# Differential attention: mixing the two softmax maps before the first one is normalized

## The chip, the cores and the metric

The kernel runs on one core of a Trainium2 chip. The core has a matmul engine (PE, with its weight loads shown apart as PEld), a vector engine (DVE), an activation engine (ACT), a general engine (POOL) and an engine that issues transfers (SP). Each works through its own queue of instructions in order, and they meet at semaphores. The metric is the device time of one execution, in microseconds.

## The reference, cut to what matters

The whole program is a chain of four layers. The change touches the attention of the first layer: 512 tokens (256 of the context, 256 of the image), 4 heads, and in each head two pairs of queries and keys, 64 wide, that give two maps over the same values.

```
def _diff_softmax_mix(q, k, v, lam):
    s = jnp.einsum('bhmqd,bhmkd->bhmqk', q.astype(F32), k.astype(F32)) * (A_QK_DIM ** -0.5)
    p = jax.nn.softmax(s, axis=-1)
    w = p[:, :, 0] - lam * p[:, :, 1]
    return jnp.einsum('bhqk,bhkd->bhqd', w, v.astype(F32))
...
    k_all = jnp.concatenate([k_c.astype(F32), k_l], axis=3)
```

`lam` is one number, computed from four small inputs. Written with unnormalized exponentials e0, e1 and their sums s0, s1 over the keys, the mixture is w = e0 / s0 - lam * e1 / s1.

## The kernel before

The program is a row of stages; between two stages all engines meet. The stage in question is `diff_attention_stage` (from L2593). It walks through 16 units (h, q): head h of 4, block q of 4 with 128 queries each. Blocks 0 and 1 see all 512 keys, blocks 2 and 3 only the last 256 (`first_key`). All data is float32.

For each unit, and each on its engine:
- `score` (PE, L2642): two products, one for each map, queries of the block against the keys, into banks 2 * (u % 2) + m.
- `maxima` (DVE, L2722, L2723): the row maxima of both maps, times the negative scale.
- `exps` (ACT, L2686): the exponentials of both maps into `prob`, with their row sums in columns 2 and 3 of `stat`.
- L2736 to L2738 (DVE): inverses of the two sums into columns 4 and 5; the second times `net.LAM` (which holds minus lam); the second map times this column, in place. `link` makes DVE wait for its own last instruction.
- L2742 (DVE): first map times column 4, plus the second map: `mixed`.
- L2668 (PE): `mixed` is transposed in tiles of 128x128 into bank 4 + u % 2, by `nc.tensor.transpose` with the identity matrix of the constants.
- L2702 (ACT): the bank is copied to `mixed_t`.
- `weigh` (PE, L2652): values times `mixed_t`, summed over key tiles into bank 6; once a head DVE copies the bank to `OT` (L2751, the last one L2754).

The order is written out by hand in each engine's loop. PE runs scores two units ahead and weighs one unit behind:

```
            for u, (h, q) in enumerate(units):
                if u + 2 < len(units):
                    score(u + 2)
                pe.wait_ge(mixed_ready, u + 1)
...
                if u:
                    weigh(u - 1)
                for n in hosted[u]:
                    mod.add(pe, n, first_slot)
```

The stage hosts other work in its gaps. `Modulation` streams the matrices of the layers' modulation, 1 MB at a time, through a ring of four places: SP fetches (L432) when PE has used a place; `mod.add` on PE first folds the sums before (`fold`, L456) and then takes one block (L443, 16 small products); `mod.copy` on ACT (L451) brings the sums out of the bank. Three blocks come before unit 0 and then one for each of the units 1 to 15. ACT copies the block of unit u - 1 at the start of its loop for unit u. Besides, POOL sums neighbouring tokens for the next stages (L2628 to L2631) in the first part of the stage, ACT damps a tile (L2710) and DVE adds them (`shift`, L2729), from unit 2 and 3 on. In the loop of unit u ACT's order is: modulation copy, copy of the turned mixture of u, exponentials of u + 2, damping. DVE's order is: inverses and mixture of u, maxima of u + 2, shift, and the copy of the output where a head ends.

Of the kernel before, what the change touches and what calls it, by code (L numbers as in the profile page):

```python
# [29 lines left out]
ALU = mybir.AluOpType  # L30
ACT = mybir.ActivationFunctionType
# [3 lines left out]
P = 128  # L35
# [3 lines left out]
TOK = 512  # L39
# [14 lines left out]
C_IDENT, C_ONES, C_BLK, C_LE, C_GE = (P * n for n in range(5))  # L54
# [2538 lines left out]
def diff_attention_stage(net, mod, first_slot, last_slot):  # L2593
# [4 lines left out]
    nc = net.nc  # L2598
    near = [net.HT[:, t, :] for t in range(KT)] + [net.PT[:, t, :] for t in range(26, 32)]
    values = net.SC[:, 0:2048].rearrange("p (t m) -> p t m", m=512)  # L2600
    prob = net.SC[:, 2048:4096].rearrange("p (b m k) -> p b m k", b=2, m=2)
    mixed = net.SC[:, 4096:5120].rearrange("p (b k) -> p b k", b=2)
    mixed_t = net.SC[:, 5120:6144].rearrange("p (b k) -> p b k", b=2)
    stat = net.SC[:, 6144:6144 + 8 * 16].rearrange("p (u n) -> p u n", n=8)
    units = [(h, q) for h in range(4) for q in range(NCH)]
    first_key = lambda q: 0 if q < 2 else 2
    scale = 64 ** -0.5
    with Stage(net, "diff_attention") as st:
        scored, max_ready, exp_ready = st.sem("scored"), st.sem("max_ready"), st.sem("exp_ready")
        mixed_ready, turned, turned_copied = st.sem("mixed_ready"), st.sem("turned"), st.sem("turned_copied")  # L2610
        out_ready, out_taken, own = st.sem("out_ready"), st.sem("out_taken"), st.sem("dve_own")
        near_ready, damped = st.sem("near_ready"), st.sem("damped")
        ahead = range(first_slot, first_slot + 3)
        upto = [first_slot + 3 + (last_slot - first_slot - 2) * u // 16 for u in range(len(units) + 1)]
        hosted = [range(upto[u], upto[u + 1]) for u in range(len(units))]

        @st.sync
        def _(sp):
            for n in range(first_slot + SLOTS, last_slot + SLOTS + 1):
                sp.wait_ge(mod.summed, n - SLOTS + 1)  # L2620
                mod.fetch(sp, n)
# [11 lines left out]
        @st.tensor  # L2633
        def _(pe):
            def score(u):
                h, q = units[u]
                if u >= 2:
                    pe.wait_ge(exp_ready, 2 * (u - 1))
                k0 = first_key(q) * P
                for m in range(2):  # L2640
                    rows = slice(64 * m, 64 * m + 64)
                    last = nc.tensor.matmul(net.ps[2 * (u % 2) + m][:, k0:TOK], net.PT[rows, h, P * q:P * q + P],  # L2642
                                            net.PT[rows, 4 + h, k0:TOK], start=True, stop=True)
                last.then_inc(scored, 1)

            def weigh(u):
                h, q = units[u]
                pe.wait_ge(turned_copied, u + 1)
                if q == 0 and h:
                    pe.wait_ge(out_taken, h)  # L2650
                for t in range(first_key(q), NCH):
                    last = nc.tensor.matmul(net.ps[6][:, P * q:P * q + P], values[:, t, P * h:P * h + P],  # L2652
                                            mixed_t[:, u % 2, P * t:P * t + P],
                                            start=(t == first_key(q)), stop=(t == NCH - 1))
                last.then_inc(out_ready, 1)

            score(0)
            score(1)
            for n in ahead:
                mod.add(pe, n, first_slot)  # L2660
            for u, (h, q) in enumerate(units):
                if u + 2 < len(units):
                    score(u + 2)
                pe.wait_ge(mixed_ready, u + 1)
                if u >= 2:
                    pe.wait_ge(turned_copied, u - 1)
                for t in range(first_key(q), NCH):
                    last = nc.tensor.transpose(net.ps[4 + u % 2][:, P * t:P * t + P],  # L2668
                                               mixed[:, u % 2, P * t:P * t + P], net.const(C_IDENT))
                last.then_inc(turned, 1)  # L2670
                if u:
                    weigh(u - 1)
                for n in hosted[u]:
                    mod.add(pe, n, first_slot)
            weigh(len(units) - 1)
            mod.fold(pe, last_slot, first_slot)

        @st.scalar
        def _(act):
            def exps(u):  # L2680
                k0 = first_key(units[u][1]) * P
                act.wait_ge(max_ready, u + 1)
                if u >= 2:
                    act.wait_ge(mixed_ready, u - 1)
                for m in range(2):
                    act.activation(prob[:, u % 2, m, k0:TOK], net.ps[2 * (u % 2) + m][:, k0:TOK], ACT.Exp,  # L2686
                                   bias=stat[:, u, m:m + 1], scale=scale,
                                   accum_out=stat[:, u, 2 + m:3 + m]).then_inc(exp_ready, 1)

            mod.copy(act, ahead[0])  # L2690
            exps(0)
            mod.copy(act, ahead[1])
            exps(1)
            mod.copy(act, ahead[2])
            for u, (h, q) in enumerate(units):
                k0 = first_key(q) * P
                for n in hosted[u - 1] if u else ():
                    mod.copy(act, n)
                act.wait_ge(turned, u + 1)
                if u >= 2:  # L2700
                    act.wait_ge(out_ready, u - 1)
                act.activation(mixed_t[:, u % 2, k0:TOK], net.ps[4 + u % 2][:, k0:TOK],  # L2702
                               ACT.Copy).then_inc(turned_copied, 1)
                if u + 2 < len(units):
                    exps(u + 2)
                t = u - 2
                if t >= 0:
                    f = net.PT[:, 12 + t, :]
                    act.wait_ge(near_ready, 3 * (t + 1))
                    act.activation(f, f, ACT.Copy, scale=net.DER[:, 14 + t:15 + t]).then_inc(damped, 1)  # L2710
            for n in hosted[-1]:
                mod.copy(act, n)

        @st.vector
        def _(dve):
            link = Chain(dve, own)

            def maxima(u):
                k0 = first_key(units[u][1]) * P
                dve.wait_ge(scored, u + 1)  # L2720
                for m in range(2):
                    link(nc.vector.reduce_max(stat[:, u, m:m + 1], net.ps[2 * (u % 2) + m][:, k0:TOK], AX_X))  # L2722
                nc.vector.tensor_scalar(stat[:, u, 0:2], stat[:, u, 0:2], -scale, None,  # L2723
                                        ALU.mult).then_inc(max_ready, 1)

            def shift(t):
                f = net.PT[:, 12 + t, :]
                dve.wait_ge(damped, t + 1)
                nc.vector.scalar_tensor_tensor(f, near[t], net.DER[:, t:t + 1], f, ALU.mult, ALU.add)  # L2729

            maxima(0)
            maxima(1)
            for u, (h, q) in enumerate(units):
                k0 = first_key(q) * P
                dve.wait_ge(exp_ready, 2 * (u + 1))
                link(nc.vector.reciprocal(stat[:, u, 4:6], stat[:, u, 2:4]))  # L2736
                link(nc.vector.tensor_tensor(stat[:, u, 5:6], stat[:, u, 5:6], net.LAM[:, 0:1], ALU.mult))
                link(nc.vector.tensor_scalar(prob[:, u % 2, 1, k0:TOK], prob[:, u % 2, 1, k0:TOK],  # L2738
                                             stat[:, u, 5:6], None, ALU.mult))
                if u >= 2:  # L2740
                    dve.wait_ge(turned, u - 1)
                nc.vector.scalar_tensor_tensor(mixed[:, u % 2, k0:TOK], prob[:, u % 2, 0, k0:TOK], stat[:, u, 4:5],  # L2742
                                               prob[:, u % 2, 1, k0:TOK], ALU.mult, ALU.add).then_inc(mixed_ready, 1)
                if u + 2 < len(units):
                    maxima(u + 2)
                t = u - 3
                if t >= 0:
                    shift(t)
                if q == 0 and h >= 1:
                    dve.wait_ge(out_ready, 4 * h)  # L2750
                    nc.vector.tensor_copy(net.OT[:, h - 1, :], net.ps[6][:, :]).then_inc(out_taken, 1)  # L2751
            shift(len(near) - 1)
            dve.wait_ge(out_ready, len(units))
            nc.vector.tensor_copy(net.OT[:, 3, :], net.ps[6][:, :])  # L2754
            for some in ((first_slot, 23), (24, last_slot)):
                mod.bias(dve, (first_slot, last_slot), *some)
# [1433 lines left out]
```

## Time and profile before

| What | Value |
|---|---|
| median of 3 runs | 2049.76 us (2048.55 to 2051.72) |
| profiled execution | 2046.13 us |
| its span in the profile | 2044.3 us |
| PE busy in the span | 1846.4 us (90%) |
| DVE busy | 1245.1 us (61%) |
| ACT busy | 860.7 us (42%) |
| POOL busy | 285.4 us (14%) |
| mean granted clock of PE | 0.968 |
| the stage `diff_attention` | from 201.0 to 275.4 us |

Busy time is that of instructions in flight; matmuls overlap, so a busy PE is not PE at its peak. Most of the program is large matmuls in other stages; the stage of the change is 3.6% of the span. Times in the rows are counted from the span's start.

### The profile page before, as it was taken

What the parts mean: (1) busy time and instruction counts of PE and PEld (TensorE: products, weight loads), DVE (VectorE), ACT (ScalarE), POOL (GpSimd) and SP (SyncE); (2) the same over time, 40 slices, a digit from 0 to 9 for tenths busy, and PEclk for the clock granted to TensorE, in tenths of its full rate; (3) what the DMA queues carried; (4) which work ended last, traced back from release to release, by engine and by line L of the source; (5) the groups of instructions that cost most, each with busy time, mean ns of one, the idle gap of its engine ahead of it and who ended that gap; (6) DMA issues with size and microseconds to landing.
All of it is one profiled execution on the core that took longest, in us unless ns stands there. A gap on an engine that the chain in (4) does not pass through costs nothing. (4 is left out here: it accounts for less than half of the span.)

```text
span 2044.3 us, 42257 instructions
## 1 busy us (share of the span) xinstructions
PE 1846.4 (90%) x18096; PEld 1613.2 (79%) x18096; DVE 1245.1 (61%) x2155; ACT 860.7 (42%) x1592; POOL 285.4 (14%) x341
## 2 busy tenths in 40 slices
PE   7998787667789999999999779999889999979997
PEld 5786545556659888888978679999679999769997
DVE  4565857465565642453565868855667756667743
ACT  4321567335243321221334555534554445464432
POOL 0200303305113000002200420012021012021001
PEclk8999987989989999999999999999999999999998
DMA  9752751020052323232331055555225556225543
GB/s 319 207 165 83 229 171 36 4 64 4 4 176 72 108 98 97 89 103 83 108 100 41 22 187 182 189 187 165 83 83 191 181 167 205 83 83 180 190 149 101
DMA packets 249004, 255.04 MB, mean 125 GB/s; under 512 B 6914, under 2 KB 247186, under 8 KB 248690
## 3 DMA queue, kind: packets, MB, share of 16 engines
q1 hardware_dynamic: 239214, 242.85, 36.9%
q10 hardware_dynamic: 8740, 8.51, 1.3%
q8 instruction: 143, 2.34, 0.5%
q0 software_dynamic: 864, 0.98, 0.4%
q14 instruction: 43, 0.35, 0.1%
HBM read 251.28 MB, written 1.05 MB: 123 GB/s over the span
## 5 line engine op out<-in xcount | busy, mean ns | idle before, releaser
L529 DVE TENSOR_TENSOR RING_rounded<-RING,SC_rounded 128x1024 fp32r<-128x1024 f32 (+2 forms) x390 | 461.3, 1225 | 217.6 <-ACT SC_rounded L522 217.3
L549 PE MATMUL bank<-OT_rounded,SC_rounded 128*128 128x256 f32 (+1 forms) x1808 | 574.6, 318 | 15.1 <-DVE HT_rounded L1113 6.8
L550 PE MATMUL bank<-HT_rounded,SC_rounded 128*128 128x256 f32 (+1 forms) x1808 | 569.7, 315 | 0.0
L551 PE MATMUL bank<-OT_rounded,RING_rounded 128*128 128x256 f32 (+1 forms) x1808 | 568.0, 314 | 0.0
L522 ACT ACTIVATE SC_rounded<-RING 128x1024 fp32r<-128x1024 f32 (+2 forms) x390 | 372.5, 1006 | 329.9 <-DMA RING<-in_l_mlp_w 185.0
L549 PEld LDWEIGHTS bank<-OT_rounded,SC_rounded 128*128 128x128 f32 x1808 | 342.4, 189 | 45.0 <-DVE HT_rounded L1113 7.6
L551 PEld LDWEIGHTS bank<-OT_rounded,RING_rounded 128*128 128x128 f32 x1808 | 341.6, 189 | 25.4
L550 PEld LDWEIGHTS bank<-HT_rounded,SC_rounded 128*128 128x128 f32 x1808 | 342.1, 189 | 21.7
L549 PE MATMUL bank<-PT_rounded,SC_rounded 128*128 128x256 f32 (+1 forms) x896 | 277.6, 310 | 4.8 <-DVE RING_rounded L529 4.8
L550 PE MATMUL bank<-PT_rounded,SC_rounded 128*128 128x256 f32 (+1 forms) x896 | 277.2, 309 | 0.0
L551 PE MATMUL bank<-PT_rounded,RING_rounded 128*128 128x256 f32 (+1 forms) x896 | 275.9, 308 | 0.0
L549 PEld LDWEIGHTS bank<-PT_rounded,SC_rounded 128*128 128x128 f32 x896 | 168.5, 188 | 16.7 <-DVE RING_rounded L529 6.0
L551 PEld LDWEIGHTS bank<-PT_rounded,RING_rounded 128*128 128x128 f32 x896 | 168.2, 188 | 10.6
L550 PEld LDWEIGHTS bank<-PT_rounded,SC_rounded 128*128 128x128 f32 x896 | 168.4, 188 | 9.5
L550 PE MATMUL bank<-OT_rounded,SC_rounded 128*128 128x256 f32 (+1 forms) x336 | 101.4, 302 | 0.0
L549 PE MATMUL bank<-HT_rounded,SC_rounded 128*128 128x256 f32 (+1 forms) x272 | 84.4, 310 | 15.3 <-DVE OT_rounded L1464 6.6
L3349 DVE TENSOR_TENSOR SC<-SC,bank 128x512 f32<-128x512 f32 (+1 forms) x80 | 51.3, 683 | 68.0 <-PE bank L3230 67.5
L795 DVE SCALAR_TENSOR_TENSOR XT<-bank,MOD,XT 128x256 f32<-128x256 f32 x48 | 21.3, 479 | 115.3 <-PE bank L551 115.3
L551 PE MATMUL bank<-HT_rounded,RING_rounded 128*128 128x256 f32 (+1 forms) x272 | 83.2, 306 | 0.0
L775 ACT ACTIVATE PT<-bank 128x512 f32<-128x512 f32 x32 | 18.9, 598 | 123.7 <-PE bank L551 123.7
L549 PEld LDWEIGHTS bank<-HT_rounded,SC_rounded 128*128 128x128 f32 x272 | 52.6, 193 | 19.1 <-DVE RING_rounded L529 12.2
L836 DVE TENSOR_TENSOR PT<-PT 128x512 f32<-128x512 f32 x32 | 22.1, 690 | 74.7 <-ACT PT L775 74.7
(561 smaller groups left out, 2787.8 us busy)
## 6 DMA issues: line engine op xcount, KB each, us to landing
RING<-in_l_mlp_w SPq DMA_DIRECT2D x64, 1024.0 KB, 5.3
RING<-in_w_ffn_in SPq DMA_DIRECT2D x44, 1024.0 KB, 5.1
RING<-in_l_mod_w SPq DMA_DIRECT2D x32, 1024.0 KB, 6.1
RING<-in_l_w_in SPq DMA_DIRECT2D x25, 1024.0 KB, 5.4
RING<-in_w_ffn_out SPq DMA_DIRECT2D x16, 768.0 KB, 4.3
RING<-in_w_in SPq DMA_DIRECT2D x10, 1024.0 KB, 5.4
RING<-in_w_ffn_out SPq DMA_DIRECT2D x16, 640.0 KB, 3.9
PT<-in_l_mod_w SPq DMA_DIRECT2D x8, 1024.0 KB, 10.1
```

What stands on the lines that cost most here:

```text
L522: act.activation(net.high4(s, m)[:, 0:self.w.kts[s], :], net.ring_half(net.RING, s, m, self.w.kts[s]), ACT.Copy).then_inc(self.high_ready, 1)
L529: net.nc.vector.tensor_tensor(low, whole, net.high4(s, m)[:, 0:self.w.kts[s], :].bitcast(F32), ALU.subtract).then_inc(self.split_ready, 1)
L549: net.nc.tensor.matmul(bank[:, tokens], high, x_high, start=start, stop=False)
L550: net.nc.tensor.matmul(bank[:, tokens], high, x_low, start=False, stop=False)
L551: return net.nc.tensor.matmul(bank[:, tokens], low, x_high, start=False, stop=stop)
L775: act.activation(hidden.whole[:, 2 * q + m, :], part.bank(q, m)[:, :], ACT.Relu).then_inc(part.taken, 1)
L795: return nc.vector.scalar_tensor_tensor(into, bank[:, tokens], net.MOD[:, gate + tile, j:j + 1], into, ALU.mult, ALU.add)
L836: link(nc.vector.tensor_tensor(whole, whole, whole, ALU.mult))
L3349: nc.vector.tensor_tensor(inv, inv, bank, ALU.subtract).then_inc(doubled, 1)
```

## The change

The mixture is taken as s0 * w instead of w: with r = -lam * s0 / s1 it is e0 + r * e1, so the second map no longer needs a pass of its own, and both maps stay unnormalized. The factor 1 / s0 belongs to a row of the mixture, that is to a column of the turned one. It is applied while the mixture is turned: instead of a transpose with the identity, PE multiplies `mixed` with a diagonal matrix that holds 1 / s0. ACT makes this matrix for each unit (identity times column 4 of `stat`) in one of two new buffers, `scaling`, when DVE has signalled the inverses (`inverted`); PE waits for it (`scaling_ready`) in front of the turning. On DVE, the product of the second inverse and lam takes the first sum as a further factor.

```
+    scaling = net.SC[:, 6272:6528].rearrange("p (b m) -> p b m", b=2)
...
+        inverted, scaling_ready = st.sem("inverted"), st.sem("scaling_ready")
...
+                pe.wait_ge(scaling_ready, u + 1)
                 pe.wait_ge(mixed_ready, u + 1)
                 if u >= 2:
                     pe.wait_ge(turned_copied, u - 1)
                 for t in range(first_key(q), NCH):
-                    last = nc.tensor.transpose(net.ps[4 + u % 2][:, P * t:P * t + P],
-                                               mixed[:, u % 2, P * t:P * t + P], net.const(C_IDENT))
+                    last = nc.tensor.matmul(net.ps[4 + u % 2][:, P * t:P * t + P], mixed[:, u % 2, P * t:P * t + P],
+                                            scaling[:, u % 2, :], start=True, stop=True)
...
                 for n in hosted[u - 1] if u else ():
                     mod.copy(act, n)
+                act.wait_ge(inverted, u + 1)
+                act.activation(scaling[:, u % 2, :], net.const(C_IDENT), ACT.Copy,
+                               scale=stat[:, u, 4:5]).then_inc(scaling_ready, 1)
                 act.wait_ge(turned, u + 1)
...
                 dve.wait_ge(exp_ready, 2 * (u + 1))
-                link(nc.vector.reciprocal(stat[:, u, 4:6], stat[:, u, 2:4]))
-                link(nc.vector.tensor_tensor(stat[:, u, 5:6], stat[:, u, 5:6], net.LAM[:, 0:1], ALU.mult))
-                link(nc.vector.tensor_scalar(prob[:, u % 2, 1, k0:TOK], prob[:, u % 2, 1, k0:TOK],
-                                             stat[:, u, 5:6], None, ALU.mult))
+                nc.vector.reciprocal(stat[:, u, 4:6], stat[:, u, 2:4]).then_inc(inverted, 1)
+                dve.wait_ge(inverted, u + 1)
+                link(nc.vector.scalar_tensor_tensor(stat[:, u, 6:7], stat[:, u, 5:6], net.LAM[:, 0:1], stat[:, u, 2:3],
+                                                    ALU.mult, ALU.mult))
                 if u >= 2:
                     dve.wait_ge(turned, u - 1)
-                nc.vector.scalar_tensor_tensor(mixed[:, u % 2, k0:TOK], prob[:, u % 2, 0, k0:TOK], stat[:, u, 4:5],
-                                               prob[:, u % 2, 1, k0:TOK], ALU.mult, ALU.add).then_inc(mixed_ready, 1)
+                nc.vector.scalar_tensor_tensor(mixed[:, u % 2, k0:TOK], prob[:, u % 2, 1, k0:TOK], stat[:, u, 6:7],
+                                               prob[:, u % 2, 0, k0:TOK], ALU.mult, ALU.add).then_inc(mixed_ready, 1)
```

## Rows read from the trace of the kernel before

**Rows 1.** Stretches (us): busy us of each engine (records), granted clock, DMA share, GB/s.

```profile
215.00:220.00 5.00, 2.50 (x12) 2.50 (x13) 4.83 (x8) 1.35 (x5) 5.00 (x12) 0.60 0.26 90
...
250.00:275.00 25.00, 22.25 (x228) 15.60 (x228) 20.35 (x50) 15.50 (x41) 0.00 (x0) 1.00 0.85 275
```

**Rows 2.** Waits, 195 to 285 us: who, for whom, total us, times, longest.

```profile
PEld bank L2668 <- DVE SC L2742: 17.5, 12, 4.7
```

**Rows 3.** Waits of SP's queue, 195 to 290 us.

```profile
SPq L432 <- PE bank L443: 73.5, 19, 12.7
```

**Rows 4.** Groups of instructions, 200 to 277 us: busy us, mean ns, idle before.

```profile
L2652 PE MATMUL bank<-SC 128*128 128x128 f32 x96 | 14.3, 288 | 0.0
...
L2668 PE MATMUL bank<-CONST,SC 128*128 128x128 f32 x48 | 9.2, 304 | 11.6 <-DVE SC L2742 11.6
L2738 DVE TENSOR_SCALAR SC<-SC 128x512 f32<-128x512 f32 (+1 forms) x16 | 8.7, 541 | 0.6
```

**Rows 5.** Timeline of PE, steady part: start us, us, engine, line, records [idle before].

```profile
250.73 0.66 PE L2668 MATMUL bank<-CONST,SC 128*128 128x128 f32 x4 [0.74 <-DVE SC L2742]
...
251.22 1.06 PE L2652 MATMUL bank<-SC 128*128 128x128 f32 x8
...
254.61 0.44 PE L2668 MATMUL bank<-CONST,SC 128*128 128x128 f32 x2
...
254.88 1.06 PE L2652 MATMUL bank<-SC 128*128 128x128 f32 x8
...
256.21 1.07 PE L443 MATMUL bank<-RING,SC 128*32 128x256 f32 x16
...
257.21 1.13 PE L2642 MATMUL bank<-PT 64*128 64x512 f32 x4
...
258.27 0.44 PE L2668 MATMUL bank<-CONST,SC 128*128 128x128 f32 x2
...
266.12 0.66 PE L2668 MATMUL bank<-CONST,SC 128*128 128x128 f32 x4 [0.74 <-DVE SC L2742]
...
271.55 0.44 PE L2668 MATMUL bank<-CONST,SC 128*128 128x128 f32 x2
```

**Rows 6.** Timeline of ACT and DVE, the same part.

```profile
251.42 0.60 ACT L2702 ACTIVATE SC<-bank 128x512 f32<-128x512 f32 x1 [1.43 <-PE bank L2668]
...
252.81 0.73 ACT L2710 ACTIVATE PT<-PT,DER 128x512 f32<-128x512 f32 x1
...
254.73 1.42 DVE L2722 TENSOR_REDUCE SC<-bank 128x1 f32<-128x512 f32 x2 [1.23 <-PE bank L2642]
...
256.38 0.69 ACT L2686 ACTIVATE SC<-bank,SC 128x512 f32<-128x512 f32 x1 [0.91 <-DVE SC L2723]
...
257.72 0.71 ACT L2710 ACTIVATE PT<-PT,DER 128x512 f32<-128x512 f32 x1
...
258.33 0.38 ACT L451 ACTIVATE SC<-bank 128x256 f32<-128x256 f32 x1
```

**Rows 7.** Groups of ACT by shape, whole execution.

```profile
L3714 ACT ACTIVATE PT<-bank,LORA 128x128 f32<-128x128 f32 x16 | 4.8, 445 | 0.0
...
L3743 ACT ACTIVATE RING<-RING 128x128 f32<-128x128 f32 x4 | 1.6, 394 | 0.0
...
L1769 ACT ACTIVATE PT<-bank 128x128 f32<-128x128 f32 x4 | 1.1, 280 | 30.1 <-PE bank L1704 30.1
```

**Rows 8.** Timeline of DVE and PE, first units.

```profile
208.69 1.45 DVE L2738 TENSOR_SCALAR SC<-SC 128x512 f32<-128x512 f32 x1
...
211.89 0.66 PE L2668 MATMUL bank<-CONST,SC 128*128 128x128 f32 x4 [1.55 <-DVE SC L2742]
...
217.50 1.12 PE L2668 MATMUL bank<-CONST,SC 128*128 128x128 f32 x4 [4.32 <-DVE SC L2742]
...
223.83 0.44 PE L2668 MATMUL bank<-CONST,SC 128*128 128x128 f32 x2
...
227.49 0.44 PE L2668 MATMUL bank<-CONST,SC 128*128 128x128 f32 x2
```

## The prediction, made before the changed kernel ran

> **What bounds the kernel now.** The change sits in one stage, so I read that stage alone. First the busy time of each engine in it: between 250 and 275 us PE is busy 22.25 of 25 us and DVE 20.35, ACT only 15.50 [rows 1]. Two engines are nearly full and the third has room on average; averages don't say which one a step waits for, so next come the waits: PE's weight loads stood 17.5 us before the turning (L2668), always for the mixture of DVE (L2742) [rows 2]. Weights from memory are no limit: SP waits 73.5 us for PE to free a place of the ring, and the DMA engines are at 0.85 [rows 1, 3].
>
> Then the timeline, for the order of work. One unit (a head, a block of queries) takes on PE: score two units ahead, turn, weigh the unit before, fold, add. A head has two units with 512 keys ("wide") and two with 256 ("narrow"). From the turn of 250.73 (unit 9) to that of 266.12 (unit 13), one head, it is 15.39 us [rows 5]: 3.88 to the turn at 254.61, 3.66 to the one at 258.27, and 7.85 for the last two steps. PE's own work fills the first two. In the turn at 266.12 the row itself names DVE's mixture as what was waited for. ACT never sets the pace.
>
> **The change, part by part.**
>
> *Removed: a pass of DVE over the second map.* L2738, 16 times, 8.7 us busy together [rows 4]. Two of them are drawn out at the start (1.45 us, [rows 8]); the others have 0.41 on average, 1.7 us in a head. PE would get its mixture that much earlier. That is a gain only where nothing else is late next.
>
> *Exchanged on DVE: a product on one column for another with a second factor.* Same engine, same tiny shape; I take no difference, and a few hundredths of a microsecond at 16 units either way stay below 1 us.
>
> *PE: matmuls in place of transposes.* A transpose leaves one record (48 in L2668), a product of the same shape two (96 in L2652 for 48 products) [rows 4]. Four transposes move the following work on by 0.49 us (250.73 to 251.22); eight records of L2652 and the four of the fold take 1.33 (254.88 to 256.21); then add takes 1.00 and a wide score 1.06 [rows 5]. Of the 1.33 I count 0.44 for the fold's four, so 0.89 for eight product records, 0.11 each. With 0.06 for the first pair, a wide turn becomes 0.95 instead of 0.49, a narrow one 0.50 instead of 0.28 (254.61 to 254.88): plus 0.46 and 0.22, or 1.4 us a head. Bounds: nothing, if this operand streams as in a transpose; and the whole of it, since shape and type are those of L2652, which is why I take it.
>
> The Trainium skill (TensorE: Matmul & The Clock Gate, Terms) calls transpose mode four times faster for FP32. The rows make it twice: 0.11 us for a transposed tile, 0.22 for a multiplied one. By the rule the change would cost 0.33 us for each of 48 tiles, by the rows 0.11.
>
> *ACT: a diagonal for each unit*, a 128x128 activation. The row nearest in form (SBUF to SBUF) is 0.394 us, one from a bank is 0.280, one with a column for its bias 0.445 [rows 7]. I take 0.39 to its end and 0.30 to the next start, as activations overlap by a tenth (the damping of 257.72 lasts 0.71 and the next starts 0.61 later [rows 6]). In ACT's queue it stands behind the copy of the modulation rows (L451), which waits for PE's add, and behind the exponentials and the damping (L2710). The turn now waits for this chain. That is what is late next.
>
> I lay one head out. ACT's chain after a wide turn: turn 0.95, end of the last product and hand-over 0.20 (the same as 251.42 less 251.22), copy and two narrow exponentials 1.39 (251.42 to 252.81), damping 0.61, rows copied 0.29, diagonal 0.39, hand-over 0.06: 3.89 us [rows 5, 6]. After a wide score DVE is slower: its maxima start 1.18 us after the score does (the score starts 1.06 before the turn of 254.61, the maxima at 254.73), the exponentials at 256.38, the damping at 257.72; with 0.61, 0.29, 0.39 and 0.06 this is 5.52 us from the score's start, 4.46 from turn to turn [rows 5, 6]. Each step takes the longer of this and of PE's own chain:
> - step 1, wide to narrow: PE 0.95 + 0.89 + 0.44 + 1.00 + 1.06 = 4.34, ACT 3.89. It was 3.88.
> - step 2, narrow to narrow: PE 0.50 + 0.89 + 0.44 + 1.00 + 1.06 = 3.89, ACT 4.46. It was 3.66.
> - step 3, narrow to wide: PE under 3.5; the score went out 4.46 - 2.83 = 1.63 us before the turn, so ACT 5.52 - 1.63 = 3.89.
> - step 4, wide to wide: PE 3.9 at most, ACT 3.89. Steps 3 and 4 were 7.85 together.
>
> Together 16.6 instead of 15.39: plus 1.2 us a head. From the turn of unit 3 on: two heads 2.4; steps 3 and 4 once more, -0.1. The last two units have no score to hide the diagonal, for the rows can be copied only when add has ended: 0.95 + 0.89 + 0.44 + 1.12 + 0.29 + 0.45 = 4.14 and 0.50 + 0.89 + 0.44 + 1.12 + 0.29 + 0.45 = 3.69, against 5.43 for both (266.12 to 271.55): 2.4. The last turn: 0.2. **The later part loses 4.9 us.** With the diagonal at 0.28 it is 4.1, at 0.445 it is 5.2.
>
> *The start gains.* While POOL is busy (5.00 of 5 us in [rows 1]), DVE's passes are drawn out: L2738 took 1.45 us at 208.69 [rows 8]. Units 0 and 1 each drop one. The first turn moves from 211.89 to about 210.5, the second from 217.50 to 214.6. The turn of unit 2 came 6.33 us after it, at 223.83, where the laid-out step is 4.34: the granted clock was 0.60 between 215 and 220 us, that is 4 of 5 us at the 1.2 GHz level, from about 216.0; PE had stood idle 4.32 us before the turn of 217.50 [rows 1, 8]. After the change this idle time is about 2.3 us (210.5, 0.95 for the turn, some 0.8 for a narrow score). Bounds:
> - the slow stretch stays where it was: from 214.6 to 216.0 at full clock, the other 2.94 at half, so turn 2 at 221.9 and turn 3 4.4 later, at 226.3 instead of 227.49: gain 1.2;
> - it goes: turn 2 at 214.6 + 4.34 = 219.0, turn 3 at 223.4: gain 4.0.
>
> An idle time of 1.55 us before the turn of 211.89 was followed by work at full clock, the one of 4.32 by the fall; 2.3 is nearer to the first, but not by so much that I leave the second out. I take 3.1.
>
> *Small things.* Two more semaphores to clear on POOL when the stage ends, one more wait in PE's queue a unit, mostly passed while PE works: 0 to 0.8 us, taken as 0. The stages behind only start later.
>
> **The sum.** 4.9 - 3.1 = +1.8 us, between +0.9 and +3.7. The profiled execution took 2046.13 us (span 2044.3), so 2047.9; the median of the runs, 2049.76, lies 3.6 above it, so in its terms 2051.6. A measurement of this kernel can tell about 0.2%, 4.1 us, from nothing.
>
> **Rivals.**
> - *DVE was the bound and its relief counts (faster).* The waits for the mixture [rows 2] speak for it. It needs both new costs gone: products at the pace of transposes, the diagonal ready before the score ends. Then steps 3 and 4 fall by about 0.7 us a head to ACT's old chain, 1.7 in the later part, and with 4.0 at the start this is -5.7: 2044. It decides from the point where ACT's chain is 0.6 us shorter than laid out. Against it: the two records of L2652. 12 in 100.
> - *ACT's chain longer, slow stretch unchanged (slower).* A diagonal of 0.5 us and 0.1 us more of waits a unit on PE and ACT give 6.5 in the later part, less 1.2: +5.3, 2055. For it: every link of the chain is a hand-over between engines. 22 in 100, with all else beyond +4.1 but the next.
> - *A product four times a transpose.* As a mechanism: 0.44 us a tile for 0.11, a wide turn 1.8, a narrow one 0.93. PE's chain then sets every step but one, a head takes 18.7 us and the later part loses 11.5, the start gains 2.5: +9, 2059. The records of L2652 [rows 4] deny it; the rule quoted above would have it so. 4 in 100.
> - *The forecast*, all between -1.9 and +4.1: 62 in 100. Its lower end has the diagonal hidden and the products paid (later part +2.1, start -4.0).
>
> So faster by over 0.2%: 0.12; within it: 0.62; slower: 0.26. The range for 8 in 10 runs from 2046 to 2056, from inside the faster rival to just above the slower one; the forecast's own is 2048 to 2054.
>
> **What would show it.** Right: 96 PE records of the turning, a wide turn as x8 of about 1.06 us; in the waits PE stands before the turning for ACT, no more for DVE; a head takes 16.6 us; the turn of unit 1 is at 214.6. Wrong: PE still waits for L2742, or the diagonal is ready before the score ends (then faster), or it lasts 0.5 and more (then slower); or the clock falls at another place, in the stage or behind it, since such a stretch costs half its length.

## The result, and the profile after

The changed kernel took 2057.52 us in the median of 9 runs, the kernel before 2050.69 in 9 runs beside it: 1.0037 times as long, with an interval of 1.0023 to 1.0051. Three later comparisons of the same two kernels gave 1.0029 (1.0014 to 1.0044), 1.0031 (1.0013 to 1.0049) and 1.0028 (1.0010 to 1.0046). The mean of the four is 1.0031, 6.4 us slower. The forecast was +1.8 us, or 2051.6 us, and its range ended at 2056. Of the 5.9 us between 2051.6 and 2057.5, 0.9 belong to the kernel before, whose median is 2050.69 in the nine runs and was 2049.76 in the three that the forecast was added to.

The page of the changed kernel has PE busy for 11.7 us more than before, with 48 more records, and DVE for 5.9 us less:

```profile
span 2051.6 us, 42357 instructions
## 1 busy us (share of the span) xinstructions
PE 1858.1 (91%) x18144; PEld 1621.8 (79%) x18144; DVE 1239.2 (60%) x2139; ACT 865.6 (42%) x1608; POOL 283.3 (14%) x341
```

The waits of the stage (who, for whom, total us, times, longest), which answer to [rows 2]: PE now waits before the turning (L2671) for ACT's diagonal (L2703) in nearly every unit, and for DVE's mixture (L2748) once, at the start.

```profile
PEld bank L2671 <- ACT SC L2703: 15.1, 15, 1.3
...
PE bank L2671 <- ACT SC L2703: 6.5, 12, 0.8
...
PE bank L2671 <- DVE SC L2748: 2.3, 1, 2.3
```

Groups by line, which answer to [rows 4]: the turning has 96 records where it had 48, and a diagonal takes 0.401 us.

```profile
L2671 PE MATMUL bank<-SC 128*128 128x128 f32 x96 | 15.9, 304 | 8.8 <-ACT SC L2703 6.5 <-DVE SC L2748 2.3
...
L2703 ACT ACTIVATE SC<-CONST,SC 128x128 f32<-128x128 f32 x16 | 6.4, 401 | 0.0
```

The timeline of PE over one head, which answers to [rows 5] (turns of units 9, 10, 11 and 13), and that of ACT and DVE in front of the turn of unit 11, which answers to [rows 6]:

```profile
249.41 1.16 PE L2671 MATMUL bank<-SC 128*128 128x128 f32 x8 [0.35 <-ACT SC L2703]
...
250.41 1.06 PE L2654 MATMUL bank<-SC 128*128 128x128 f32 x8
...
253.80 0.71 PE L2671 MATMUL bank<-SC 128*128 128x128 f32 x4
...
254.35 1.06 PE L2654 MATMUL bank<-SC 128*128 128x128 f32 x8
...
258.24 0.71 PE L2671 MATMUL bank<-SC 128*128 128x128 f32 x4 [0.44 <-ACT SC L2703]
...
266.11 1.16 PE L2671 MATMUL bank<-SC 128*128 128x128 f32 x8 [0.35 <-ACT SC L2703]
```

```profile
253.91 1.42 DVE L2728 TENSOR_REDUCE SC<-bank 128x1 f32<-128x512 f32 x2 [2.22 <-PE bank L2644]
...
255.57 0.69 ACT L2689 ACTIVATE SC<-bank,SC 128x512 f32<-128x512 f32 x1 [0.64 <-DVE SC L2729]
...
256.91 0.72 ACT L2716 ACTIVATE PT<-PT,DER 128x512 f32<-128x512 f32 x1
...
257.52 0.38 ACT L451 ACTIVATE SC<-bank 128x256 f32<-128x256 f32 x1
257.79 0.40 ACT L2703 ACTIVATE SC<-CONST,SC 128x128 f32<-128x128 f32 x1
```

A head takes 16.70 us (249.41 to 266.11) where it took 15.39, in steps of 4.39, 4.44 and 7.87 for the last two. Read the second fence downwards: the maxima wait for the score, the exponentials for the maxima, then damping, rows copied, diagonal, and 0.45 us after the diagonal's start the turn of 258.24 begins. DVE is idle for 2.22 us in front of its maxima, where it was for 1.23.

The first turns, which answer to [rows 8]:

```profile
210.44 1.16 PE L2671 MATMUL bank<-SC 128*128 128x128 f32 x8 [0.16 <-ACT SC L2703]
214.52 2.05 PE L2671 MATMUL bank<-SC 128*128 128x128 f32 x8 [2.29 <-DVE SC L2748]
220.41 0.71 PE L2671 MATMUL bank<-SC 128*128 128x128 f32 x4
224.85 0.71 PE L2671 MATMUL bank<-SC 128*128 128x128 f32 x4 [0.44 <-ACT SC L2703]
```

They come at the forecast's 210.5 and 214.6, and the turn of unit 3 lies 2.6 us before that of [rows 8]. So in this pair of profiles the stage behaves as laid out: later part (unit 3 to 15) 49.18 us against 44.06, its end 4.43 behind the last turn against 4.16, start (from the first score to the turn of unit 3) 2.4 us shorter, 3.0 longer in all. The spans differ by 7.3. What was to be found is the rest.

### The profile page after: what moved, and what is told of

Same layout as the page of the kernel before. It is cut to its first block and busy times, and to the rows that moved or that the text cites. A ratio compares the mean times of both kernels' runs of the same rounds, so it can differ in the third digit from the quotient of the medians.

```text
span 2051.6 us, 42357 instructions
## 1 busy us (share of the span) xinstructions
PE 1858.1 (91%) x18144; PEld 1621.8 (79%) x18144; DVE 1239.2 (60%) x2139; ACT 865.6 (42%) x1608; POOL 283.3 (14%) x341
## 6 DMA issues: line engine op xcount, KB each, us to landing
PT<-in_l_mod_w SPq DMA_DIRECT2D x8, 1024.0 KB, 10.1
```

## The experiments

**PE's part, ACT's part, DVE's part, each alone.** `products_only` puts the matmul with the constant identity into the kernel before:

```
-                    last = nc.tensor.transpose(net.ps[4 + u % 2][:, P * t:P * t + P],
-                                               mixed[:, u % 2, P * t:P * t + P], net.const(C_IDENT))
+                    last = nc.tensor.matmul(net.ps[4 + u % 2][:, P * t:P * t + P], mixed[:, u % 2, P * t:P * t + P],
+                                            net.const(C_IDENT), start=True, stop=True)
```

> PE's part alone: DVE works as before, the turning is a matmul with the identity of the constants, no diagonal. Layout by hand: 16.2 us a head, 2.4 us longer from the turn of unit 3 to that of unit 15 and 0.7 at the start, 3 us slower in all. If instead the products cost four times a transpose it is 10 us and more; if they cost nothing, 15.4 us a head and no change. In case the rest of the program suffers from the records added on PE, the part behind the stage is 4 us longer here as well.

Measured: 1.0024 (1.0009 to 1.0038), 4.9 us where 3 were expected. A head takes 16.30 us (16.2 expected), the later part 46.80 instead of 44.06. The rows of PE show wide turns (x8) that still wait for DVE's mixture:

```profile
251.53 1.16 PE L2668 MATMUL bank<-CONST,SC 128*128 128x128 f32 x8 [0.39 <-DVE SC L2742]
```

`diagonal_only` adds the diagonal and the wait for it to the kernel before, and nothing else:

```
+                pe.wait_ge(scaling_ready, u + 1)
                 pe.wait_ge(mixed_ready, u + 1)
...
+                act.wait_ge(inverted, u + 1)
+                act.activation(scaling[:, u % 2, :], net.const(C_IDENT), ACT.Copy,
+                               scale=stat[:, u, 4:5]).then_inc(scaling_ready, 1)
                 act.wait_ge(turned, u + 1)
```

> ACT's part alone: the kernel before, with a diagonal made for each unit and waited for by PE in front of the turning, which stays a transpose with the identity and doesn't use it. DVE as before. Layout by hand: 15.5 us a head against 15.4, since most of the chain fits where PE waits for DVE anyway; 1.1 us longer from the turn of unit 3 to that of unit 15, and up to 1 at the start, so the stage is 1 to 2 us longer. If ACT's chain alone were the cause of the loss, a head would be above 16 us.

Measured: 1.0013 (0.9997 to 1.0028), a head 15.48 us, the later part 45.25. So ACT's chain alone costs next to nothing in a whole head. Within it, the step from narrow to narrow takes 4.44 us, as in the changed kernel, against 3.66 before, and the two steps behind it 7.18 against 7.85. The likely reason, which no run isolates, is that PE stood waiting for DVE's mixture in those two anyway.

`relief_only` is the changed kernel without the diagonal and with the transposes:

```
-                pe.wait_ge(scaling_ready, u + 1)
...
-                act.wait_ge(inverted, u + 1)
-                act.activation(scaling[:, u % 2, :], net.const(C_IDENT), ACT.Copy,
-                               scale=stat[:, u, 4:5]).then_inc(scaling_ready, 1)
...
-                    last = nc.tensor.matmul(net.ps[4 + u % 2][:, P * t:P * t + P], mixed[:, u % 2, P * t:P * t + P],
-                                            scaling[:, u % 2, :], start=True, stop=True)
+                    last = nc.tensor.transpose(net.ps[4 + u % 2][:, P * t:P * t + P],
+                                               mixed[:, u % 2, P * t:P * t + P], net.const(C_IDENT))
```

> DVE's part of the change alone: unnormalized mixing, the transposes as before, no diagonal. It leaves out the factor 1 / s0; the norm over each head's 128 outputs that follows divides it out, but for its epsilon. Layout by hand: a head takes 14.3 us (15.4 before, 16.6 after), the part from the turn of unit 3 to that of unit 15 is 3.1 us shorter than before, the start gains 3 to 5: 6 to 8 us faster than before, 2043. Rival (DVE's pass was hidden all along): 15.4 us a head and at most 3 us faster, from the start alone.

> DVE's part alone, transposes as before, factor 1 / s0 left to the norm behind, once more: the version that the experiments point to. Its stage was 5 us shorter in the profile; the first comparison gave 0.997 with an interval of 0.9953 to 0.9987. Expected again 0.997 to 0.998, 2045 to 2048 us where before is at 2051; if the rest of the program takes the gain back by its clock, no change.

Measured: 0.9970 (0.9953 to 0.9987) and, again, 0.9968 (0.9951 to 0.9984): 6 us faster than before. A head takes 14.48 us (14.3 expected) and the later part 41.30, 2.8 us less (3.1 expected); the start took 24.0 and 22.7 us. PE waits for the mixture in wide units still, but less (0.29 and 0.70 us where it was 0.74 and 1.16):

```profile
246.41 0.66 PE L2670 MATMUL bank<-CONST,SC 128*128 128x128 f32 x4 [0.29 <-DVE SC L2744]
...
250.29 0.44 PE L2670 MATMUL bank<-CONST,SC 128*128 128x128 f32 x2
...
253.96 0.44 PE L2670 MATMUL bank<-CONST,SC 128*128 128x128 f32 x2
...
260.89 0.66 PE L2670 MATMUL bank<-CONST,SC 128*128 128x128 f32 x4 [0.29 <-DVE SC L2744]
```

The price that the diff pays for this relief, products and diagonal, is what turns -6 into +6. This version beats both kernels. It leaves out the factor 1 / s0, which the norm of the next stage divides out but for its epsilon (1e-5, added to the mean square), so the output is not exactly the same.

**The diagonal out of the queue.** `diagonal_ahead` is the changed kernel with ACT's diagonal of the next unit made right behind the exponentials:

```
-                act.wait_ge(inverted, u + 1)
-                act.activation(scaling[:, u % 2, :], net.const(C_IDENT), ACT.Copy,
-                               scale=stat[:, u, 4:5]).then_inc(scaling_ready, 1)
...
                 if u + 2 < len(units):
                     exps(u + 2)
+                if u + 1 < len(units):
+                    diagonal(u + 1)
                 t = u - 2
```

> The changed kernel with ACT making the diagonal of the next unit right behind the exponentials, ahead of the damping and of the modulation copy. Layout by hand: PE's chain alone sets the wide steps and no step waits for the diagonal: 15.2 us a head (16.7 after, 15.4 before), the stage 5 to 6 us shorter than in the changed kernel, 2 to 3 shorter than before, so 0.9985. If the products on PE, not ACT's chain, are what costs, a head stays above 16 us.

Measured: 0.9994 (0.9984 to 1.0003), 2049.47 us where 0.9985 was expected. A head takes 15.42 us (15.2 expected) and the later part 44.14, against 16.70 and 49.18 with the same instructions in the changed kernel's order. The expectation that no step waits for the diagonal failed in one step of each head:

```profile
245.38 1.13 PE L2671 MATMUL bank<-SC 128*128 128x128 f32 x8 [0.47 <-ACT SC L2695]
```

ACT's rows show the diagonal (L2695) ahead of the damping (L2721) and of L451:

```profile
256.37 0.40 ACT L2695 ACTIVATE SC<-CONST,SC 128x128 f32<-128x128 f32 x1
...
256.66 0.71 ACT L2721 ACTIVATE PT<-PT,DER 128x512 f32<-128x512 f32 x1
...
257.27 0.38 ACT L451 ACTIVATE SC<-bank 128x256 f32<-128x256 f32 x1
```

So of the 5.1 us of the later part, the place in ACT's queue is worth 5.0. The products remain, and DVE's relief pays for them.

**Is the surplus behind the stage?** Both kernels as they are, once more, to see what single profiles are worth:

> The kernel before, unchanged. It shows what this comparison tells from nothing and gives a second profile of the part behind the stage. Both theories: 1.000 within 0.15%, a head of the attention stage 15.4 us, the stage's last turn at about 271.5. The part behind the stage (from the end of the attention stage to the end of the span, 1769 us in the first profile): if it wanders by chance with the places at which the clock falls, it differs here from the first profile by up to 3 us either way.

> The changed kernel, unchanged. In its first profile the stage ends 2.7 us later than before, the span is 7.3 us longer. Theory 1 (the stage is all of the loss, the rest is the clock's chance): the part behind the stage comes within 3 us of that of before_again and the ratio is 1.0015 to 1.003. Theory 2 (something behind the stage is made slower by the change, whatever it is): it is 4 us or more longer again, ratio 1.003 to 1.005.

Measured: 0.9995 (0.9979 to 1.0010) and 1.0029. The later part was 44.07 and 49.19 us, equal to the first profiles within 0.01. From the norm stage to the end of the span, work that no version changes, it was 1768.6 and 1774.1 us before, 1773.1 and 1781.0 after. The second pair lies 6.9 us apart, which is theory 2's 4 us or more, while the ratio is within theory 1's bounds. But the two profiles of the same kernel lie 5.5 and 7.9 us apart, more than the 3 us expected, so these pairs decide nothing.

Then the stage of the kernel before was made to end later, by n more copies of its last output:

```
+            for again in range(n):
+                link(nc.vector.tensor_copy(net.OT[:, 3, :], net.ps[6][:, :]))
             nc.vector.tensor_copy(net.OT[:, 3, :], net.ps[6][:, :])
```

> The kernel before, with the last copy of the attention's output (DVE, L2754) made four times more, each waiting for the one before: the stage ends about 3 us later, as in the changed kernel, and nothing else differs (no record of PE more, same results). Theory 1 (when the stages behind start 3 us later, the clock falls in other places of them): as in both profiles of the changed kernel, 17.1 us of half clock lie between 285 and 312 us instead of 10.2, the preparation of the RWKV stage gets 2 us longer, and the ratio is 1.002 to 1.0035, 4.5 to 7 us. Theory 2 (the changed instructions themselves, or their number, slow the rest): 10.2 us of half clock there and +3 us in all, 1.0015.

> The same with two copies, the stage ends 1.5 us later. Theory 1: the length of the part behind depends on where it starts, not on how much was added, so this one need not lie halfway; its profile has either 10.2 or 17.1 us of half clock behind the stage, and with 17.1 the whole is 3.5 us or more longer, with 10.2 it is 1.5. Theory 2: +1.5 us, 1.0007.

> The kernel before with the last copy of the attention's output made four times more, once more: its first 8 runs were 6 us above before with an end of the stage 3 us later. Theory 1 (the rest of the program is longer when it starts 3 us later, since the clock falls more often): again 5 to 7 us, ratio 1.0025 to 1.0035. Theory 0 (those were few runs, a delay costs what it is): 3 to 3.5 us, 1.0015.

> The same with six copies: the stage ends about 4.4 us later. Theory 1: the surplus depends on the place, not on the size of the delay; two copies (1.5 us) had none, so if places repeat every few microseconds six copies have little either, and this kernel is no slower than the one with four: +4 to +6 us. Theory 0: +4.5 us. A surplus that grows with the delay would give 9.

> The changed kernel with two such copies: its stage ends 1.5 us later still, 4.5 to 5 us after that of before. Theory 1: it leaves the bad place, so it is no slower than the changed kernel itself, +4.5 to +6 us. Theory 2 (something in the changed instructions slows the rest by 3 us whatever the place): +7.5 to +8 us, 1.0037 or more.

| Kernel | stage made later by | ratio | interval |
|---|---|---|---|
| 2 copies | 1.4 us | 1.0002 | 0.9989 to 1.0016 |
| 4 copies | 2.9 | 1.0037 | 1.0022 to 1.0051 |
| 4 copies, again | 2.9 | 1.0018 | 1.0003 to 1.0032 |
| 6 copies | 4.4 | 1.0029 | 1.0015 to 1.0042 |
| after with 2 copies | 1.4 beyond after | 1.0035 | 1.0018 to 1.0051 |

The first run with 4 copies cost 7.6 us for 2.9, as theory 1 has it, but its profile had 10.2 us of half clock (PE's granted clock at 0.50) between 285 and 312 us and not 17.1. The repetition had the long stretch (17.0 us) and cost 3.7, two of the four profiles of before without copies have it too, and 6 copies cost 6 us for 4.4. The changed kernel with 2 copies is 7.2 us above before, between theory 1's 4.5 to 6 and theory 2's 7.5 to 8, with an interval that holds both: this run doesn't tell a place from a fixed burden of the changed instructions.

What tells more is the granted clock, which is on record for every run. Over the 156 runs of the kernel before, a mean clock lower by 0.001 goes with 1.0 us more. So each kernel can be compared with before at equal clock (one straight line fitted through the 297 runs of these comparisons; an estimate. The first comparison is left out, since its runs of before have no clock on record):

| Kernel (runs) | granted clock | of before | mean time against before, us | at equal clock, us (error) |
|---|---|---|---|---|
| changed (27) | 0.9633 | 0.9628 | +5.5 | +6.0 (0.5) |
| products_only (12) | 0.9614 | 0.9629 | +5.1 | +3.9 (0.7) |
| diagonal_only (12) | 0.9638 | 0.9629 | +1.8 | +2.7 (0.8) |
| relief_only, both (23) | 0.9647 | 0.9630 | -5.8 | -4.0 (0.5) |
| diagonal_ahead (11) | 0.9647 | 0.9629 | -2.1 | -0.3 (0.8) |
| 2 copies (12) | 0.9649 | 0.9629 | -0.7 | +1.3 (0.8) |
| 4 copies, both (20) | 0.9617 | 0.9630 | +5.0 | +3.6 (0.6) |
| 6 copies (12) | 0.9610 | 0.9631 | +6.2 | +3.9 (0.8) |
| changed with 2 copies (12) | 0.9635 | 0.9631 | +7.5 | +7.8 (0.8) |

At equal clock a delay costs about what it is: 1.3, 3.6 and 3.9 us for 1.4, 2.9 and 4.4. The rest of what the copies showed goes with the clock. And the changed kernel's clock is no lower than that of before, so the clock explains none of its loss. By the same measure about 2 of the 6 us of `relief_only` go with a higher clock. Whether a stage that ends at another time causes another clock isn't shown.

**Is it in the start?** One profile of this series showed something else. With 4 copies, again, the stage's start, which these copies don't touch, was 5.5 us shorter than in the first profile of before:

```profile
208.99 0.66 PE L2668 MATMUL bank<-CONST,SC 128*128 128x128 f32 x4
...
213.09 1.12 PE L2668 MATMUL bank<-CONST,SC 128*128 128x128 f32 x4 [2.81 <-DVE SC L2742]
218.49 0.44 PE L2668 MATMUL bank<-CONST,SC 128*128 128x128 f32 x2
222.16 0.44 PE L2668 MATMUL bank<-CONST,SC 128*128 128x128 f32 x2
```

Against [rows 8] the turn of unit 1 is 4.4 us early. The passes of DVE in front of the first turn differ, with the same instructions on DVE and POOL. First the profile of before, then this one:

```profile
207.50 1.15 DVE L2737 TENSOR_TENSOR SC<-SC,LAM 128x1 f32<-128x1 f32 x1
208.69 1.45 DVE L2738 TENSOR_SCALAR SC<-SC 128x512 f32<-128x512 f32 x1
210.17 1.67 DVE L2742 SCALAR_TENSOR_TENSOR SC<-SC 128x512 f32<-128x512 f32 x1
```

```profile
206.42 0.16 DVE L2737 TENSOR_TENSOR SC<-SC,LAM 128x1 f32<-128x1 f32 x1
206.62 1.20 DVE L2738 TENSOR_SCALAR SC<-SC 128x512 f32<-128x512 f32 x1
207.85 0.75 DVE L2742 SCALAR_TENSOR_TENSOR SC<-SC 128x512 f32<-128x512 f32 x1
```

Four more profiles followed, two of each kernel.

> The kernel before once more, for its profile. Between the start of the attention stage and the turn of unit 3, profiles with DVE's and POOL's work as before have shown 20.9 to 26.4 us (mean of six 25.0). Theory S (the start gains less than the first two profiles showed, since before's start is often short too): this profile has less than 25 us there. Theory R (the start gains 2.4 us, the surplus of the changed kernel lies in the rest): 26 us, and a rest behind the stage of 1769 to 1774 us.

> The changed kernel once more. From the turn of unit 3 to that of unit 15 it is 49.2 us whatever the theory. Theory S: 24 to 25 us in front of it. Theory R: 24.0, and a rest behind the stage of 1776 us and more.

> As the third look at before: theory S, the start varies and is below 25 us in about half of the looks; theory R, 26 us.

> As the third look at the changed kernel: theory S, 24 to 25 us at the start and a rest like that of before; theory R, 24.0 and a rest of 1776 us and more.

The third profile of the changed kernel has a start of the long kind:

```profile
212.76 1.37 PE L2671 MATMUL bank<-SC 128*128 128x128 f32 x8
218.09 2.05 PE L2671 MATMUL bank<-SC 128*128 128x128 f32 x8 [3.32 <-DVE SC L2748]
224.97 0.71 PE L2671 MATMUL bank<-SC 128*128 128x128 f32 x4
229.42 0.71 PE L2671 MATMUL bank<-SC 128*128 128x128 f32 x4 [0.44 <-ACT SC L2703]
```

Its stretches, with the granted clock as the figure after the busy times (POOL busy all through 205 to 220):

```profile
210.00:215.00 5.00, 4.76 (x32) 2.41 (x24) 3.36 (x5) 1.79 (x6) 5.00 (x12) 0.68 1.09 357
215.00:220.00 5.00, 1.91 (x9) 1.94 (x10) 4.83 (x8) 1.30 (x5) 5.00 (x12) 0.67 0.44 141
220.00:225.00 5.00, 5.00 (x34) 3.33 (x33) 0.83 (x2) 2.18 (x7) 0.57 (x3) 0.65 0.00 0
```

All profiles of the two kernels, those with copies at the end included, from the first score to the turn of unit 3, with the time at half clock in this stretch:

| Start as in | start, us (half clock, us) | mean |
|---|---|---|
| before (8 profiles) | 26.4 (10.2), 25.9 (10.2), 26.8 (13.7), 25.8 (10.1), 26.3 (13.7), 20.9 (3.4), 24.3 (6.8), 26.0 (10.2) | 25.3 |
| after (5 profiles) | 24.0 (6.7), 24.1 (6.8), 27.5 (13.7), 24.1 (6.8), 24.9 (8.4) | 24.9 |

Neither theory came as laid out. Theory S wanted less than 25 us in half of the new profiles of before: they were 26.8 and 25.8. Theory R wanted a rest of 1769 to 1774 us in them, and it was 1776.5 and 1777.4. Over all, the start gains 0.4 us by the means, with an error of 0.9, and 1.9 by the medians (26.0 and 24.1): 3.1 lies three errors away, 2.4 two. What orders the values is the half clock. A straight line through the thirteen starts has 0.51 us for each microsecond at half clock, and at equal half clock the changed kernel's start is 0.3 us longer, with an error of 0.4 (an estimate from the table). The two typical starts, 26 us and 24, differ by 10.2 and 6.8 us at half clock.

The part from the norm stage on is 1775.0 us on average in the eight and 1777.0 in the five, each with an error of 1.4 to 1.5: 2 us more, with an error of 2. It too goes with the clock: over all eighteen profiles it ran from 1768.5 us with 111 us at half clock to 1782.3 with 144.

## Why the prediction was wrong

**Steps that held.** The change does move the limit of the turning from DVE to ACT and PE. Products at 0.22 us a tile: the turning has 96 records, and from the narrow turn of 253.80 to the weighing of 254.35 there are 0.55 us (0.50 forecast). The diagonal: 0.401 us (0.39). ACT's chain as what is late next: PE's weight loads wait for L2703 in 15 units, step by step 4.39, 4.44 and 7.87 against 4.34, 4.46 and 7.78. A head: 16.70 (16.6). The later part and what lies behind the last turn: 5.1 + 0.3 = 5.4 us where 4.9 stood. The parts taken alone gave 16.30, 15.48 and 14.48 us a head, and `diagonal_ahead` shows that the diagonal's place in ACT's queue is the cause: with the same instructions 5.0 of the 5.1 us are gone. The step from wide to narrow is PE's own, as laid out: 4.39 us in the changed kernel and in `products_only`.

**The rule of the Trainium skill** (TensorE: Matmul & The Clock Gate, Terms), transposes four times faster for FP32, does not agree with this case: the rows make it two, 0.11 us for a transposed tile and 0.22 for a multiplied one, and `products_only` lost 2.7 us in the later part, not 10 us and more. The rival built on that factor had a slip of its own: by the terms of the prediction its head is 18.3 us at most, not 18.7. Nothing else hangs on it.

**The step that failed** is "I take 3.1" for the start: a term read from one profile of before, whose start is of the long kind, from what two dropped passes would be worth there, and from two bounds for the slow stretch. In the one profile that it was worked out for, the first turns came within 0.1 us, but the slow stretch did neither what the one bound said (it stays where it was) nor what the other said (it goes): the clock fell at 214.3 us instead of 216.0, and came back after 3.4 us instead of 6.8. The turn of unit 2 came 5.89 us after that of unit 1, where the two bounds had 7.3 and 4.4, and 2.4 us were gained. The argument that an idle time of 2.3 us speaks against a fall was wrong there: 2.29 us of idle time stood before the turn of 214.52. The stretches of the changed kernel, with the granted clock in the same place as in [rows 1]; 0.73 between 215 and 220 us is 2.7 us at half clock, where 0.60 was 4:

```profile
210.00:215.00 5.00, 2.55 (x18) 1.78 (x15) 4.70 (x9) 2.18 (x8) 5.00 (x12) 0.93 1.02 345
215.00:220.00 5.00, 5.00 (x40) 4.05 (x38) 3.17 (x5) 2.02 (x7) 4.68 (x12) 0.73 0.29 96
```

Above all, the start is not a fixed length. It was 20.9 to 26.8 us with the work of before and 24.0 to 27.5 with that of after. It goes with the time at half clock, and the same three passes of DVE took 2.1 us in the shortest and 4.3 in the first profile, while POOL worked. Mean against mean, the gain is 0.4 us, and at equal half clock there is none. The passes that remain are drawn out beside POOL too: in the changed kernel the product on one column took 0.99 us there (0.22 later) and the mixing of unit 0 1.72 (0.75 later). With 0.4 and the later part's 5.4 the sum is 5.0 instead of 1.8, 2055: just inside the range, and beyond what was called no change.

**What stays open.** 6.4 us were measured. With the mean start 5.0 of them are accounted for, with the medians 3.5; the error of the start is 0.9, that of the rest, which the prediction put at nothing, 2. At equal clock the account closes better: 5.4 + 0.3 = 5.7 us from the stage's rows, 6.0 (error 0.5) from the runs. That the clock falls more often behind the changed stage is not borne out: its mean granted clock is 0.9633 against 0.9628. Why the start's slow stretch is often shorter in the changed kernel is open, and so is which comes first there, the slow passes or the slow clock. Both kernels without POOL's sums at the start, which would settle the start's share, were not tried.

In the rivals' terms, the outcome is nearest to "ACT's chain longer, slow stretch unchanged", +5.3 us. Its size came by luck: the diagonal took 0.40 us and not 0.5, the chain was as long as the forecast had it (5.4, not 6.5), the slow stretch changed, and the start's gain was what was missing.

## What to carry to other kernels

When work is taken off an engine that others wait for and given to one with room, lay out the new chain through that engine's queue: what stands ahead of the new instruction counts, not its 0.4 us; moved ahead of the damping and the copy of the modulation rows, it held PE up by 0.47 us in one step of a head, and the later part was as long as before the change. A scale factor by rows in front of a norm over the same rows needs no instruction at all, if the norm's epsilon may weigh a little differently. A gain in a stretch whose length varies from profile to profile should be read from several profiles, or be taken as zero. And where the clock varies, the granted clock of each run belongs beside its time.

## What was not expected of the hardware

- The product of two columns with a third factor takes 0.22 us in the steady part; the one with two factors took 0.16.
- The same instructions at the start of the stage took from 20.9 to 26.8 us, and the length goes with PE's time at half clock in it: 3.4 us at 20.9, 6.8 at 24.3, about 10.2 around 26, 13.7 at 26.8; 6.8 at 24.1 and 13.7 at 27.5 in the changed kernel. Which of the two is the cause isn't shown.
- The preparation stage that comes next but one, whose work no version changes, took 42.7 to 43.1 us (to the first instruction of the stage behind it) in nine of the eighteen profiles and 45.0 to 45.2 in the other nine, with about 28 and 34.5 us at half clock. In the first nine the clock fell 0.8 to 1.6 us after the stage began and came back after 6.8; in the others it fell after 0.1 to 0.7 and stayed low for 17.1. Four of the five profiles of the changed kernel are among the long ones, and three of the eight of before.
